# A ring of five places for U and ten for V, with row constants loaded per tile

## The chip, the cores and the metric

The kernel runs on one core of a Trainium2 chip. The metric is the device time of one execution in microseconds. A core has five engines, each with an instruction stream of its own: TensorE (PE, matrix products), VectorE (DVE), ScalarE (ACT), GpSimd (POOL) and SyncE (SP). Sixteen DMA engines serve the core; here GpSimd issues the gathers and SyncE nearly all the other loads. The engines meet only through semaphores.

## The reference, cut to what matters

Two transformer-like layers over one sequence of 512 tokens, width 1024, in float32. Layer 1 mixes with an S5 state space model and a banded attention, layer 2 with a compressed and a windowed attention and a short convolution. Each layer ends in the same step, which sets most of the traffic: every token picks 8 x 16 = 128 of 16384 experts, and each expert is one row of `u_tab` and one of `v_tab` (4 KB each).

```python
def block_fn(args):
    xb, eb, gb = args
    a = jnp.einsum('cd,ced->ce', xb, u_tab[eb]).astype(jnp.float32)
    w = (gb * jax.nn.gelu(a, approximate=False)).astype(xb.dtype)
    return jnp.einsum('ce,ced->cd', w, v_tab[eb])
```

`xb` is the normed row of the token times a row of gains: `ln2_g` in layer 1, and in layer 2 `ln_ffn_g_2` times one plus a modulation row, with another modulation row added. The output of layer 2 is normed once more with `ln_final_g_2`.

## The kernel before, in words

The tokens are cut into four tiles of 128, one token per partition, and the program goes through eight tiles in order: n = 0 to 3 are layer 1, n = 4 to 7 are layer 2 on the same tokens. A tile needs 128 **slots**; slot s = 128 n + k handles expert k of all 128 tokens of tile n. There are 1024 slots (`NSLOT`), and each engine's stream has a part for a slot:

- GpSimd gathers the U and the V row of the slot for every partition in one indirect DMA of 8 KB per partition, 1.05 MB in all (L1944). `both_rows(s)` gives the destination in the tile `ring`.
- VectorE multiplies U with the token's row and sums (`dot`, L372), which writes `aw`.
- ScalarE applies GELU and makes a diagonal matrix of the weights (`weigh`, `diag`; four buffers for diagonals, two slots at a time).
- TensorE adds diagonal times V into PSUM (`vmm`, L1472, 8 matmuls per slot). It takes V of slot c - `VL` when its stream is at slot c; `VL` is 4.

The ring has `NU` = 4 places for U and `NV` = 8 for V, so the gather of slot s waits for `dot(s - 4)` and for `vmm(s - 8)`, which is in TensorE's stream at its slot s - 4.

Beside the slots each stream holds the dense work of the *next* tile. `L1_PARTS` and `L2_PARTS` give the order and the width in slots: in layer 1 norm 4, win 25, qk 7, mid 52, branch 14, route 11, top 15; in layer 2 norm 4, win 30, conv 7, cmp 17, att 36, wout 7, route 12, top 15. `pace(n, part, f)` emits all slots that are due before that point of the part, so the position of each dense instruction among the slots is written into the stream of each engine, and every engine runs its stream strictly in order. In `mid` four groups g of 13 slots each do a head group of the attention and a quarter of the state space model. There TensorE comes in group g to `T.wait_ge("a_pt1", n, g)` at 13 g + 9 and waits until VectorE, in its own stream, has reached the copy of L678 (`att_pt`) at about the same slot.

The dense weights come through `wsl`, six buffers of two 128 x 512 blocks (`NWS`, 512 KB a unit). SyncE issues unit k when unit k - 6 has been used; `extra(k)`, called ahead of unit k, issues whatever other load belongs there, some after a wait. All of SyncE's loads are in one stream too. In layer 2 the units of a tile are 24 of `win`, 8 of `wout`, 8 of `wq` and 1 of `sk`; TensorE takes them in pairs (`project`), one slot between two pairs.

The constant rows lie in SBUF tiles of their own before the change: `rowA` holds the gain row of `route` (loaded once a layer), `gt1` the modulation row of the output projection (a part of `pers`, loaded once), `finr` the row of the last norm (loaded once). `fin`, 4 KB per partition, holds the output tile of layer 2 between `finish` and the store, parts of the state space work in layer 1, and half of the scores of `route`. `finish2(n - 1)` (the last norm's product) is emitted at slot `VL` + 4 of a tile. `kT1` holds the keys of all four tiles of layer 1.

Of the kernel before, what the change touches and what calls it, by code (L numbers as in the profile page):

```python
# [9 lines left out]
F32 = mybir.dt.float32  # L10
# [5 lines left out]
W1 = 384  # L16
NU = 4
NV = 2 * NU
NWS = 6
NSLOT = 1024  # L20
PAIR = 2
VL = 4
END = NSLOT + VL + 6

# [75 lines left out]
def build(nc, A, out, act_counts):  # L100
    ctx = ExitStack()
    with ctx:
# [50 lines left out]
        gt2 = sb("gt2", [128, D])  # L153
        finr = sb("finr", [128, D])
        xT = sb("xT", [128, 8, 128])
# [3 lines left out]
        cols3 = sb("cols3", [128, 2, 8])  # L159
        rowA = sb("rowA", [128, D])  # L160
        rowB = sb("rowB", [128, D])
        big = sb("big", [128, 5120])
        pers = sb("pers", [128, 13312])
        rflat = ring[:, :, :].rearrange("p a b -> p (a b)")
# [3 lines left out]
        L2d = nc.dram_tensor("L2d", [8, 16, W1], F32, kind="Internal").ap()  # L168
        modd = nc.dram_tensor("modd", [12, 512], F32, kind="Internal").ap()
        modr = modd.rearrange("(a b) c -> a (b c)", b=2)  # L170

# [10 lines left out]
        bias1, o = carve(pers, o, 16, 256)  # L182
        kT1, o = carve(pers, o, 2, 512)
        v1, o = carve(pers, o, 2, 256)
# [4 lines left out]
        snk, o = carve(pers, o, 16)  # L189
        assert o <= 13312, o  # L190

# [36 lines left out]
        zprev, o = carve(pers, o, 512)  # L228
        gt1, o = carve(pers, o, 1024)
        at_route = o  # L230
# [25 lines left out]

        rsc2 = finr[:, :]
        bmod = finr[:, 256:768].rearrange("p (b c) -> p b c", c=128)

        def route_bufs(blk):  # L260
            if blk:
                sS, o = carve(pers, at_route, 16, 128)
                halves, base = [sS[:, 0:8, :], sS[:, 8:16, :]], pers
            else:
                halves = [x[:, :].rearrange("p (a b) -> p a b", b=128) for x in (fin, gt2)]
                base, o = rowB, 0
            r = {"halves": halves}
            r["s2"], p = carve(base, o, 256)
            r["cand"], p = carve(base, p, 16, 16)
            r["oh"], o = carve(base, o, 2, 16, 16)  # L270
# [4 lines left out]
            assert o <= (13312 if blk else D), o  # L275
            return r
# [18 lines left out]
        assert o <= 3328  # L295
        mrow = [finr[:, 0:128], finr[:, 128:256]]
        first = [carve(rflat, 512 * k, 4, 128)[0] for k in range(3)]
# [64 lines left out]
        def vector_program(v):  # L362
# [28 lines left out]
            def finish2(n):  # L391
                V.stage("fin")
                V.wait_ge("fsq", n)
                V(v.tensor_scalar(st[:, 2:3], st[:, 2:3], 1.0 / D, 1e-6, ALU.mult, ALU.add))
                V.wait_own()
                V(v.reciprocal(st[:, 2:3], st[:, 2:3]), ("frc", n))
                V.wait_ge("frs", n)
                V.wait_ge("finr")
                V(v.scalar_tensor_tensor(fin[:, :], fin[:, :], st[:, 2:3], finr[:, :], ALU.mult, ALU.mult),
                  ("fout", n))  # L400

            def slots(x):
                back = V.here
                while V.slot < x and V.slot < END:
                    c = V.slot
                    V.slot += 1
                    n, k = divmod(c, 128)
                    if c < NSLOT:
                        dot(c)
                    if k == VL + 2 and n >= 1:  # L410
                        finish(n - 1)
                    if k == VL + 4 and n >= 5:
                        finish2(n - 1)
                V.stage(back)
# [156 lines left out]
            def qk1(n):  # L571
                i = n
                pace(n, "qk", 0.0)
                if n:
# [22 lines left out]
                V.wait_ge("kT_t", n)  # L597
                V(ts(kT1[:, :, 128 * i:128 * i + 128], PS[2][:, 0:256].rearrange("p (a b) -> p a b", a=2), kgc,
                     None, ALU.mult, None), ("kT", n))
# [181 lines left out]
            def route(n):  # L781
                i, blk, b = n % 4, n // 4, n % 2
                X = xn[:, b, :]
                pace(n, "route", 0.0)
                V.stage("route")
                rstd(n, "r", 1, D)
                if n == 4:
                    V.wait_ge("lnf")
                    V.wait_ge("modrow", 4)
                    V(v.scalar_tensor_tensor(rowA[:, :], rsc2, 1.0, rowA[:, :], ALU.add, ALU.mult), ("rowA", 1))  # L790
                    V.wait_own()
                if n == 0:
                    V.wait_ge("rowA", 0)
                V(v.scalar_tensor_tensor(X, hres[:, i, :], st[:, 1:2], rowA[:, :], ALU.mult, ALU.mult),
                  *([] if blk else [("X", n)]))
# [12 lines left out]
                pace(n, "route", 1.0)  # L808
# [238 lines left out]
            def wout2(n):  # L1047
# [19 lines left out]
                for b in range(2):  # L1067
# [4 lines left out]
                    V.wait_ge("wout", n, b)  # L1072
                    V.wait_ge("modrow", 2)
                    V(tt(x, PS[4 + b], gt1[:, 512 * b:512 * b + 512], ALU.mult), ("wo_e", n, b))
# [48 lines left out]
        def scalar_program(a):  # L1123
# [58 lines left out]
            def slots(x):  # L1182
                back = S.here
                while S.slot < x and S.slot < END:
# [7 lines left out]
                    if k == VL + 3 and n >= 5:  # L1192
                        finish(n - 1)
                    if k == VL + 4 and n >= 5:
                        finish2(n - 1)
# [118 lines left out]
            def route(n):  # L1314
# [141 lines left out]
        def tensor_program(t):  # L1456
# [143 lines left out]
            def scores1(n, g):  # L1600
# [8 lines left out]
                for r in range(4):  # L1609
                    k0 = 128 * (n - 1) + s0  # L1610
                    x = t.matmul(PS[r // 2][:, 256 * (r % 2) + s0:256 * (r % 2) + 256],
                                 xT[64 * a_:64 * a_ + 64, 4 * m + r, :],
                                 kT1[64 * a_:64 * a_ + 64, m, k0:128 * (n + 1)], start=True, stop=True)
                T(x, ("a_sc", n, g))
# [334 lines left out]
        def sync_program(s):  # L1949
# [20 lines left out]
            def extra(k):  # L1970
# [7 lines left out]
                if (n, name, b, u) == (0, "glu", 0, 0):  # L1978
                    load(rowA[:, :], A["ln2_g"].broadcast_to([128, D]), "rowA", 0)
                    load(shm[:, :, :], A["k_shift"], "shm")  # L1980
# [28 lines left out]
                if n >= 4 and (name, b, u) == ("win", 4, 0):  # L2009
                    Y.wait_ge("h", n - 1, 1)  # L2010
                    Q(s.dma_start(cw, A["conv_w_2"][0, :, 0, :].unsqueeze(0).broadcast_to([128, 3, 512])), "cw",
                      ("cw", n))
# [9 lines left out]
                if (n, name, b, u) == (5, "win", 0, 0):  # L2022
                    Y.wait_ge("rowA", 1)
                    load(finr[:, :], A["ln_final_g_2"].unsqueeze(0).broadcast_to([128, D]), "finr")

# [144 lines left out]
```

## Time and profile before

| | us |
|---|---|
| median of 3 runs | 3549.24 |
| lowest and highest | 3537.84, 3552.84 |
| the profiled execution | 3552.45 |
| its span | 3551.0 |
| PE busy | 2498.8 |
| DVE busy | 2390.7 |
| ACT busy | 1370.3 |
| POOL busy | 1078.5 |

The span goes from the first to the last instruction of the profiled execution. The program moved 1343.61 MB at a mean of 378 GB/s. A "DMA share" is the mean busy share of the 16 DMA engines; packets of two queues overlap a little in the records, so that a full stretch reads 1.00 to 1.02. Slots start at about 285 us; before that the first tile's dense work runs alone. In a timeline row the figures are start, length, engine, line, operation and, in brackets, how long the engine sat idle before it and what ended that.

### The profile page before, as it was taken

To read this page: it belongs to the slowest core of one execution; us is meant where nothing else is said; L and a number is where in the kernel's file an instruction comes from. 1 tells how busy PE (TensorE), PEld (TensorE's weight loads), DVE (VectorE), ACT (ScalarE), POOL (GpSimd) and SP (SyncE) were. 2 spreads that over 40 slices of the span, in tenths; PEclk is the share of its full clock that TensorE was granted. 3 is DMA by queue.
4 is the path that set the end of the run, shared out by engine and by line. 5 is a ranking of instruction groups with operands and counts; after the bars stand their busy time and mean duration, and the time that the engine had idled before them with its cause. 6 is when DMAs were issued, how large, how long until landed. Compare 5 with 4: busy or idle time off the path is not lost.

```text
span 3551.0 us, 40113 instructions
## 1 busy us (share of the span) xinstructions
PE 2498.8 (70%) x13640; PEld 977.6 (28%) x13640; DVE 2390.7 (67%) x5690; ACT 1370.3 (39%) x3648; POOL 1078.5 (30%) x1038
## 2 busy tenths in 40 slices
PE   7768669676696776866577667767677668765555
PEld 3433233222332223322222223222232223311111
DVE  7438873687835878467664886668775887666664
ACT  1113332344323443233283335534383436533332
POOL 0001332223322233332333323332333323333332
PEclk9689779798797987988778888888888888977777
DMA  7659999999999999999999999999999999999998
GB/s 241 218 200 375 369 355 406 416 408 393 359 396 416 416 391 355 385 394 396 380 409 395 399 398 394 395 400 414 374 401 393 393 394 401 387 386 393 396 407 336
DMA packets 228013, 1343.61 MB, mean 378 GB/s; under 512 B 28360, under 2 KB 33768, under 8 KB 95968
## 3 DMA queue, kind: packets, MB, share of 16 engines
q0 software_dynamic: 148320, 1076.50, 76.0%
q1 hardware_dynamic: 78816, 262.43, 19.3%
q8 instruction: 107, 1.75, 0.2%
q10 hardware_dynamic: 672, 2.12, 0.1%
q14 instruction: 98, 0.80, 0.1%
HBM read 1338.24 MB, written 2.71 MB: 378 GB/s over the span
## 4 chain that ended last, share of the span: by engine, by line
DMA 31%; PE 26%; DVE 17%; issue 15%; POOL 5%; ACT 4%; SPq 0%; POOLq 0%; ACTq 0%; DVEq 0%
DMA ring<-in_k_uv,idx 15%; PE ps L1543 12%; DMA ring<-in_k_vu,idx 12%; PE ps L1472 9%; DVE ring L372 6%; POOL ring L1944 5%; DMA wsl<-in_k_wu 4%; DVE big L420 2%; ACT L1128 1%; PE ps L1525 1%; PE ps L1681 1%; DVE rowB L420 1%; ACT diag L1128 1%; ACT xr L1128 1%; PE ps L1627 1%
## 5 line engine op out<-in xcount | busy, mean ns | idle before, releaser
L372 DVE CUSTOM_DVE_ANT_0 ring<-ring,xn 128x1024 f32<-128x1024 f32 x1024 | 1243.7, 1222 | 654.3 <-DMA ring<-in_k_uv,idx 351.7
L1472 PE MATMUL ps<-ring,diag 64*64 64x512 f32 x8192 | 1272.2, 741 | 518.9 <-ACT diag L1128 474.9
L1944 POOL DMA_INDIRECT ring<-in_k_vu,idx x512 | 530.7, 1036 | 1267.2 <-DVE aw L372 673.7
L1944 POOL DMA_INDIRECT ring<-in_k_uv,idx x512 | 541.7, 1058 | 1109.5 <-DVE aw L372 855.9
L1543 PE MATMUL ps<-wsl,xT 128*128 128x512 f32 (+1 forms) x1536 | 730.1, 622 | 77.9 <-DMA wsl<-in_k_wu 54.1
L1472 PEld LDWEIGHTS ps<-ring,diag 64*64 64x64 f32 x8192 | 304.8, 158 | 1240.8 <-ACT diag L1128 725.2
L1128 ACT ACTIVATE aw<-aw 128x2 f32<-128x2 f32 x512 | 103.9, 203 | 1320.1 <-DVE aw L372 1314.6
L1128 ACT ACT_TABLE_LOAD x375 | 481.1, 1283 | 64.2 <-DVE big L420 51.8
L1543 PEld LDWEIGHTS ps<-wsl,xT 128*128 128x128 f32 x1536 | 291.7, 200 | 528.1 <-issue 437.8
L1128 ACT ACTIVATE diag<-gid,aw 128x64 f32<-128x64 f32 x1024 | 306.3, 341 | 129.6 <-PE ps L1472 112.9
L1128 ACT ACTIVATE gid<-ident,gate 128x64 f32<-128x64 f32 x1024 | 292.5, 332 | 0.0
L1681 PE MATMUL ps<-pers,rowB 128*128 128x64 f32 x224 | 51.3, 421 | 106.1 <-DVE rowB L678 81.6
L1525 PE MATMUL ps<-ident,big 128*128 128x128 f32 x288 | 60.1, 332 | 81.9 <-DVE big L420 31.7
L420 DVE TENSOR_TENSOR big<-ps,big 128x512 f32<-128x512 f32 x40 | 27.6, 690 | 107.6 <-PE ps L1543 107.3
L1525 PE MATMUL ps<-ident,xr 128*128 128x128 f32 x208 | 37.1, 334 | 85.7 <-DVE xr L424 64.4
L372 DVE DVE_READ_ACCUMULATOR2_ANT aw<- 128x1 f32 x1024 | 83.9, 82 | 0.0
L1681 PEld LDWEIGHTS ps<-pers,rowB 128*128 128x128 f32 x224 | 48.7, 329 | 118.4 <-issue 118.4
L1525 PEld LDWEIGHTS ps<-ident,big 128*128 128x128 f32 x288 | 38.0, 164 | 137.3 <-ACT big L1128 60.6
L1128 ACT ACTIVATE xr<-ps 128x512 f32<-128x512 f32 x32 | 18.2, 589 | 144.6 <-PE ps L1543 141.1
L420 DVE TENSOR_TENSOR big<-big 128x512 f32<-128x512 f32 x84 | 58.2, 693 | 20.0 <-ACT big L1128 17.1
L1863 PE MATMUL ps<-pers,big 128*128 128x64 f32 x320 | 48.9, 288 | 23.9 <-DVE big L1024 23.9
L420 DVE TENSOR_TENSOR big<-ps,pers 128x512 f32<-128x512 f32 (+5 forms) x120 | 58.1, 494 | 3.5 <-PE ps L1627 2.8
(227 smaller groups left out, 2033.9 us busy)
## 6 DMA issues: line engine op xcount, KB each, us to landing
wsl<-in_k_wu SPq DMA_DIRECT2D x408, 512.0 KB
wsl<-in_k_wmod SPq DMA_DIRECT2D x48, 512.0 KB
ring<-in_k_vu,idx POOLq DMA_INDIRECT x512
ring<-in_k_uv,idx POOLq DMA_INDIRECT x512
wsl<-in_k_wu SPq DMA_DIRECT2D x16, 280.0 KB
big<-in_b_gate SPq DMA_DIRECT2D x4, 1024.0 KB, 11.7
big<-in_conv_w SPq DMA_DIRECT2D x4, 768.0 KB
hres<-in_x SPq DMA_DIRECT2D x4, 512.0 KB, 7.7
```

The costliest lines, as they stand in the source:

```text
L372: V(v.tensor_tensor_reduce(u_row(s), u_row(s), xn[:, b, :], 1.0, 0.0, ALU.mult, ALU.add, aw[:, b, k:k + 1]), ("dot", s))
L420: return v.tensor_tensor(out, a_, b_, op)
L1128: return a.activation(out, in_, f, **kw)
L1472: r = t.matmul(PA[half][64 * q:64 * q + 64, :], diag[64 * half:64 * half + 64, s % (2 * PAIR), :], v_row(s)[64 * half:64 * half + 64, 512 ...
L1525: r = t.transpose(PS[bank][:, j * 128:(j + 1) * 128], s_, ident[:, :])
L1543: r = t.matmul(PS[bank][:, 0:nn], lhsT(kk_), wsl[:, at % NWS, j, 0:nn], start=(kk_ == 0), stop=(kk_ == nk - 1))
L1627: x = t.matmul(PS[2 + b][:, 256 * h + 128 * z:256 * h + 128 * z + 128], BT[32 * j:32 * j + 32, 4 * z + c, :], uT[32 * j:32 * j + 32, c, :] ...
L1681: x = t.matmul(PS[4 + h // 8][:, 64 * (h % 8):64 * (h % 8) + 64], PT1[:, r, 128 * k:128 * k + 128], v1[:, (n + 1 + k) % 2, 64 * g:64 * g + ...
L1863: r = t.matmul(PS[4 + br][:, 64 * h:64 * h + 64], PT2[:, k % 2, 128 * j:128 * j + 128], vsn[:, j, 128 * br + 64 * g:128 * br + 64 * g + 64 ...
L1944: Q(p.indirect_dma_start(out=both_rows(s), out_offset=None, in_=tab, in_offset=bass.IndirectOffsetOnAxis(ap=idx[:, n % 2, k:k + 1], axis=0 ...
```

## The change

`NU` goes from 4 to 5, `NV` = 2 `NU` with it from 8 to 10, and `VL` from 4 to 5. The gather of slot s now waits for `dot(s - 5)` and `vmm(s - 10)`, and the latter stands in TensorE's stream at its slot s - 5. The three more places of 4 KB per partition come from elsewhere: `rowA` and `finr` are gone, and `pers` shrinks from 13312 to 12192 elements.

- The row of `route` is now `lnr`, a name for `fin`, loaded ahead of the first `wq` unit of every tile: 8 loads of 512 KB in place of 2. VectorE waits for it at the start of `route`. In tile 4 VectorE makes the product with the modulation row and ScalarE writes it to DRAM (`lnd`, 4 KB); tiles 5 to 7 load it from there.
- `gt1` lies in scratch space and is loaded in each tile of layer 2, ahead of the fifth `wout` unit and after a wait of SyncE for `o1`, the end of the attention: 4 loads in place of 1.
- The row of the last norm goes to `xr` or to `wsl`: 3 loads in place of 1, two of them ahead of the 17th `win` unit of tiles 6 and 7 with a wait for `perm`, the end of an earlier tile's sum. `finish2` moves to slot 20.
- `kT1` keeps two tiles of keys; for even n the score matmul over 256 columns becomes two over 128.

```diff
-NU = 4
+NU = 5
 NV = 2 * NU
+PERS = 12192
-VL = 4
+VL = 5
...
-                    if k == VL + 4 and n >= 5:
+                    if k == (20 if n < 8 else VL + 4) and n >= 5:
                         finish2(n - 1)
...
                 rstd(n, "r", 1, D)
+                V.wait_ge("lnr", n)
                 if n == 4:
-                    V.wait_ge("lnf")
                     V.wait_ge("modrow", 4)
-                    V(v.scalar_tensor_tensor(rowA[:, :], rsc2, 1.0, rowA[:, :], ALU.add, ALU.mult), ("rowA", 1))
+                    V(v.scalar_tensor_tensor(lnr, rsc2, 1.0, lnr, ALU.add, ALU.mult), ("lnf",))
...
+                if n == 4:
+                    S.wait_ge("lnf")
+                    Q(a.dma_start(lnd, lnr[0:1, :]), "lnd", ("lnd",))
...
+                    if n % 2:
+                        x = t.matmul(PS[r // 2][:, 256 * (r % 2):256 * (r % 2) + 256], q,
+                                     kT1[64 * a_:64 * a_ + 64, m, :], start=True, stop=True)
+                    else:
+                        for k in range(s0 // 128, 2):
+                            x = t.matmul(PS[r // 2][:, 256 * (r % 2) + 128 * k:256 * (r % 2) + 128 * k + 128], q,
+                                         kT1[64 * a_:64 * a_ + 64, m, 128 * (1 - k):256 - 128 * k],
+                                         start=True, stop=True)
...
-                    load(rowA[:, :], A["ln2_g"].broadcast_to([128, D]), "rowA", 0)
...
-                    load(rsc2, modr[4:5, :].broadcast_to([128, 1024]), "modrow", 4)
-                    Y.wait_ge("X", 3)
-                    load(rowA[:, :], A["ln_ffn_g_2"].broadcast_to([128, D]), "lnf")
...
-                    load(gt1, modr[2:3, :].broadcast_to([128, 1024]), "modrow", 2)
...
+                if n >= 4 and (name, b, u) == ("wout", 1, 0):
+                    Y.wait_ge("o1", n, 1)
+                    Q(s.dma_start(gt1, modr[2:3, :].broadcast_to([128, 1024])), "gt1", ("gt1", n))
+                    if n == 4:
+                        load(rsc2, modr[4:5, :].broadcast_to([128, 1024]), "modrow", 4)
+                if (name, b, u) == ("wq", 0, 0):
+                    if n < 4:
+                        Y.wait_ge("s5b", n, 1)
+                        row = A["ln2_g"]
+                    elif n == 4:
+                        Y.wait_ge("gate", 3, 7)
+                        row = A["ln_ffn_g_2"]
+                    else:
+                        Y.wait_ge("lnd")
+                        if n >= 6:
+                            Y.wait_ge("out", n - 2)
+                        row = lnd
+                    Q(s.dma_start(lnr, row.broadcast_to([128, D])), "lnr", ("lnr", n))
+                if n >= 6 and (name, b, u) == ("win", 4, 0):
+                    last_row(n - 2)
+
+            def last_row(*tiles):
+                if tiles[0] < 6:
+                    Y.wait_ge("perm", tiles[0])
+                Q(s.dma_start(finr(tiles[0]), A["ln_final_g_2"].unsqueeze(0).broadcast_to([128, D])), "finr",
+                  *[("finr", n) for n in tiles])
```

## Rows read from the trace of the kernel before

**Rows 1.** the page: busy share of the 16 DMA engines in 40 slices; SyncE's queue.

```profile
DMA  7659999999999999999999999999999999999998
...
q1 hardware_dynamic: 78816, 262.43, 19.3%
```

**Rows 2.** windows by stage: PE, PEld, DVE, ACT, POOL busy; TensorE clock, DMA share, GB/s.

```profile
375.00:529.00 154.00, 95.10 (x650) 46.76 (x650) 123.65 (x225) 56.88 (x178) 53.02 (x52) 0.77 0.92 362
...
829.00:979.00 150.00, 95.28 (x656) 45.67 (x656) 123.53 (x226) 58.41 (x180) 53.91 (x53) 0.77 0.93 369
...
1278.00:1432.00 154.00, 97.30 (x664) 47.49 (x664) 122.69 (x224) 57.16 (x177) 56.34 (x53) 0.76 0.91 358
...
1879.00:1949.00 70.00, 55.91 (x280) 21.84 (x280) 33.24 (x59) 21.06 (x64) 23.08 (x19) 0.95 0.97 389
...
1949.00:2105.00 156.00, 104.44 (x504) 35.22 (x504) 129.99 (x384) 61.30 (x164) 47.79 (x48) 0.88 1.01 407
...
2105.00:2180.00 75.00, 48.91 (x386) 23.04 (x389) 49.76 (x102) 23.54 (x79) 27.21 (x27) 0.77 0.92 366
...
2268.00:2341.00 73.00, 60.66 (x304) 22.86 (x296) 35.57 (x68) 24.74 (x71) 23.71 (x20) 0.92 0.98 393
...
2498.00:2572.00 74.00, 48.88 (x379) 23.08 (x379) 49.95 (x104) 22.52 (x75) 28.60 (x27) 0.77 0.93 367
...
2663.00:2738.00 75.00, 61.65 (x307) 23.50 (x306) 36.12 (x68) 24.85 (x71) 22.74 (x20) 0.91 0.99 392
...
2895.00:2970.00 75.00, 49.83 (x380) 23.28 (x380) 51.09 (x108) 23.66 (x76) 30.30 (x27) 0.77 0.94 370
...
3062.00:3130.00 68.00, 57.20 (x292) 21.86 (x284) 32.79 (x60) 23.33 (x69) 24.20 (x20) 0.95 0.93 360
...
3130.00:3440.00 310.00, 172.22 (x940) 40.96 (x944) 214.09 (x522) 103.25 (x334) 122.89 (x118) 0.74 0.99 399
...
3440.00:3520.00 80.00, 44.78 (x256) 10.13 (x248) 39.26 (x63) 19.18 (x76) 29.64 (x32) 0.76 1.01 415
```

**Rows 3.** waits of GpSimd, 285 to 3551 us: total, times, longest.

```profile
POOL ring L1944 <- DVE aw L372: 1529.6, 605, 34.2
POOL ring L1944 <- PE ps L1472: 538.3, 213, 16.4
```

**Rows 4.** timeline of one stall: start, length, engine, operation, idle before it.

```profile
436.20 0.94 POOL L1944 DMA_INDIRECT ring<-in_k_vu,idx  x1 [1.06 <-DVE aw L372]
...
437.43 3.65 PE L1681 MATMUL ps<-pers,rowB 128*128 128x64 f32 x16 [9.40 <-DVE rowB L678]
...
441.01 4.77 PE L1472 MATMUL ps<-ring,diag 64*64 64x512 f32 x32
...
443.80 0.94 POOL L1944 DMA_INDIRECT ring<-in_k_vu,idx  x1 [6.67 <-DVE aw L372]
```

**Rows 5.** window of two microseconds in that stall.

```profile
444.00:446.00 2.00, 2.00 (x21) 0.62 (x14) 1.97 (x3) 0.82 (x3) 1.70 (x2) 1.00 0.43 74
```

**Rows 6.** timeline of a stall in the convolution stage of a second-layer tile.

```profile
2113.53 1.22 DVE L372 CUSTOM_DVE_ANT_0 ring<-ring,xn 128x1024 f32<-128x1024 f32 x1
...
2115.03 1.68 POOL L1944 DMA_INDIRECT ring<-in_k_vu,idx  x1 [4.63 <-DVE aw L372]
```

**Rows 7.** timeline of the output projection of tile 5.

```profile
2268.25 0.69 DVE L420 TENSOR_TENSOR big<-big 128x512 f32<-128x512 f32 x1
...
2286.21 0.69 DVE L420 TENSOR_TENSOR xr<-ps,pers 128x512 f32<-128x512 f32 x1 [4.23 <-PE ps L1543]
...
2287.13 3.70 PE L1543 MATMUL ps<-wsl,xT 128*128 128x512 f32 x8
...
2299.66 1.28 DVE L794 SCALAR_TENSOR_TENSOR xn<-hres,st,rowA 128x1024 f32<-128x1024 f32 x1 [1.16 <-ACT st L1128]
```

**Rows 8.** DMA issues: count, size, median us from issue to landing.

```profile
finr<-in_ln_final_g SPq DMA_DIRECT2D x1, 512.0 KB, 15.8
```

**Rows 9.** groups of TensorE in the middle stage of tile 2: busy, mean ns.

```profile
L1611 PE MATMUL ps<-pers,xT 64*128 64x256 f32 x24 | 6.0, 389 | 0.0
```

More of the change, by code:

```diff
@@ L153, in build @@
         gt2 = sb("gt2", [128, D])
-        finr = sb("finr", [128, D])
         xT = sb("xT", [128, 8, 128])
@@ L159, in build @@
         cols3 = sb("cols3", [128, 2, 8])
-        rowA = sb("rowA", [128, D])
         rowB = sb("rowB", [128, D])
         big = sb("big", [128, 5120])
-        pers = sb("pers", [128, 13312])
+        pers = sb("pers", [128, PERS])
         rflat = ring[:, :, :].rearrange("p a b -> p (a b)")
@@ L169, in build @@
         modd = nc.dram_tensor("modd", [12, 512], F32, kind="Internal").ap()
+        lnd = nc.dram_tensor("lnd", [1, D], F32, kind="Internal").ap()
         modr = modd.rearrange("(a b) c -> a (b c)", b=2)
@@ L182, in build @@
         bias1, o = carve(pers, o, 16, 256)
-        kT1, o = carve(pers, o, 2, 512)
+        kT1, o = carve(pers, o, 2, 256)
         v1, o = carve(pers, o, 2, 256)
@@ L189, in build @@
         snk, o = carve(pers, o, 16)
-        assert o <= 13312, o
+        mrow = [carve(pers, o + 128 * k, 128)[0] for k in range(2)]
+        bmod, o = carve(pers, o + 256, 4, 128)
+        assert o <= PERS, o
         gt, o = carve(big, 0, 2048)
@@ L228, in build @@
         zprev, o = carve(pers, o, 512)
-        gt1, o = carve(pers, o, 1024)
         at_route = o
@@ L248, in build, with finr @@
         tmp2, o = carve(big, o, 512)
+        gt1, _ = carve(big, o2 + 1024, 1024)
+        lnr = fin[:, :]
+        def finr(n):
+            return xr[:, :] if n < 6 else wsl[:, 0, :, :].rearrange("p a b -> p (a b)")
         gg = cols2[:, 0:24]
@@ L255, in build @@
         o3 = o1r.rearrange("p (h d) -> p h d", d=64)
-        rsc2 = finr[:, :]
-        bmod = finr[:, 256:768].rearrange("p (b c) -> p b c", c=128)
+        rsc2, _ = carve(big, o2, 1024)
         def route_bufs(blk):
@@ L274, in route_bufs @@
                 r[nm], o = carve(base, o, *shape, dt=dt)
-            assert o <= (13312 if blk else D), o
+            assert o <= (PERS if blk else D), o
             return r
@@ L295, in build @@
         assert o <= 3328
-        mrow = [finr[:, 0:128], finr[:, 128:256]]
         first = [carve(rflat, 512 * k, 4, 128)[0] for k in range(3)]
@@ L397, in finish2 @@
                 V.wait_ge("frs", n)
-                V.wait_ge("finr")
-                V(v.scalar_tensor_tensor(fin[:, :], fin[:, :], st[:, 2:3], finr[:, :], ALU.mult, ALU.mult),
+                V.wait_ge("finr", n)
+                V(v.scalar_tensor_tensor(fin[:, :], fin[:, :], st[:, 2:3], finr(n), ALU.mult, ALU.mult),
                   ("fout", n))
@@ L597, in qk1 @@
                 V.wait_ge("kT_t", n)
-                V(ts(kT1[:, :, 128 * i:128 * i + 128], PS[2][:, 0:256].rearrange("p (a b) -> p a b", a=2), kgc,
+                V(ts(kT1[:, :, 128 * (i % 2):128 * (i % 2) + 128], PS[2][:, 0:256].rearrange("p (a b) -> p a b", a=2), kgc,
                      None, ALU.mult, None), ("kT", n))
@@ L786, in route @@
                 rstd(n, "r", 1, D)
+                V.wait_ge("lnr", n)
                 if n == 4:
-                    V.wait_ge("lnf")
                     V.wait_ge("modrow", 4)
-                    V(v.scalar_tensor_tensor(rowA[:, :], rsc2, 1.0, rowA[:, :], ALU.add, ALU.mult), ("rowA", 1))
+                    V(v.scalar_tensor_tensor(lnr, rsc2, 1.0, lnr, ALU.add, ALU.mult), ("lnf",))
                     V.wait_own()
-                if n == 0:
-                    V.wait_ge("rowA", 0)
-                V(v.scalar_tensor_tensor(X, hres[:, i, :], st[:, 1:2], rowA[:, :], ALU.mult, ALU.mult),
+                V(v.scalar_tensor_tensor(X, hres[:, i, :], st[:, 1:2], lnr, ALU.mult, ALU.mult),
                   *([] if blk else [("X", n)]))
@@ L1072, in wout2 @@
                     V.wait_ge("wout", n, b)
-                    V.wait_ge("modrow", 2)
+                    V.wait_ge("gt1", n)
                     V(tt(x, PS[4 + b], gt1[:, 512 * b:512 * b + 512], ALU.mult), ("wo_e", n, b))
@@ L1193, in slots @@
                         finish(n - 1)
-                    if k == VL + 4 and n >= 5:
+                    if k == (20 if n < 8 else VL + 4) and n >= 5:
                         finish2(n - 1)
@@ L1609, in scores1 @@
                 for r in range(4):
[L1610 to L1613, printed above, removed]
+                    q = xT[64 * a_:64 * a_ + 64, 4 * m + r, :]
+                    if n % 2:
[6 more added lines that the diff above has]
+                                         start=True, stop=True)
                 T(x, ("a_sc", n, g))
@@ L2010, in extra @@
                     Y.wait_ge("h", n - 1, 1)
+                    if n == 5:
+                        Y.wait_ge("lnf")
                     Q(s.dma_start(cw, A["conv_w_2"][0, :, 0, :].unsqueeze(0).broadcast_to([128, 3, 512])), "cw",
@@ L2021, in extra @@
                     load(gt2[:, :], modr[5:6, :].broadcast_to([128, 1024]), "modrow", 5)
-                if (n, name, b, u) == (5, "win", 0, 0):
-                    Y.wait_ge("rowA", 1)
-                    load(finr[:, :], A["ln_final_g_2"].unsqueeze(0).broadcast_to([128, D]), "finr")
+                if n >= 4 and (name, b, u) == ("wout", 1, 0):
[23 more added lines that the diff above has]
+                  *[("finr", n) for n in tiles])
             load(hres[:, 0, :], A["x"][0, 0:128, :], "x", 0)
@@ L2041, in sync_program @@
                 unit(k)
+            for k in range(len(units) - NWS, len(units)):
+                Y.wait_ge("unit_used", k)
+            last_row(6, 7)
         for engines in ((Blank(),) * 5, (nc.vector, nc.scalar, nc.tensor, nc.gpsimd, nc.sync)):
```

## The prediction

> **What bounds the kernel now.** I read the page's slices first, for what is full nearly all the time. From the fourth slice on the 16 DMA engines are busy 90% or more of every slice but none of the compute engines is [rows 1]. Then I read the windows by stage [rows 2], because a mean hides where the DMA engines do run dry. In full stages the share reads 1.01 (1949 to 2105 us, mostly `win` of tile 5, and the closing slots, 3440 to 3520 us). In the latter only gathers run: 32 in 80 us, so one gather of 1.05 MB costs 2.5 us of all DMA engines. Against 1.01 the dry time is share lost times length [rows 2]:
>
> - `mid` of tiles 1, 2, 3: 0.09 x 154 + 0.08 x 150 + 0.10 x 154 = 41.3 us;
> - `conv` and `cmp` of tiles 5, 6, 7: 0.09 x 75 + 0.08 x 74 + 0.07 x 75 = 17.9 us;
> - `wout` and `route` of tiles 4 to 7: 0.04 x 70 + 0.03 x 73 + 0.02 x 75 + 0.08 x 68 = 11.9 us;
> - 3130 to 3440 us: 0.02 x 310 = 6.2 us.
>
> Together 77.3 us. The time after 285 us is bytes over a fixed rate plus this dry time, so an edit can win only by closing dry time, and loses by bytes.
>
> Who opens it? GpSimd waits 1529.6 us for dots and 538.3 us for TensorE's reading of V [rows 3]. Most of that is harmless: with full queues the gather of s + 4 can't be issued before the dot of s, which itself waits for data. What hurts is a gap between two issues longer than the data in flight lasts. One such gap is in [rows 4]: TensorE sits 9.40 us at L1681 until VectorE has made the copy of L678, then works off four V slots from 441.01 us on. VectorE comes late because it first has dots to do in its stream. Gathers were issued at 436.20 us and then not before 443.80 us. (The row names a dot as releaser, but the next V is free only as TensorE's block of 441.01 proceeds, so I take it as V.) From 444 to 446 us the DMA share is 0.43 and 74 GB/s move [rows 5]. `mid` has four such groups, three tiles, so 12 stalls, 41.3 / 12 = 3.4 us each. In the convolution stage VectorE itself is late: it reaches its dot at 2113.53 us behind dense work, and the next gather leaves at 2115.03 us after 4.63 us of idle GpSimd [rows 6]; there the dot is the gate. Neither kind is a rate limit: VectorE is busy 123.65 of 154 us in `mid`, 80%, and TensorE 95.10 [rows 2].
>
> **The change, part by part. The ring.** Take the stall of [rows 4]. TensorE stands at its slot P and has read V up to P - 5; before, GpSimd may gather up to P - 5 + 8 = P + 3. After, TensorE has read up to P - 6 and GpSimd may gather up to P - 6 + 10 = P + 4. Of the two places that V gains, `VL` takes one back. The dot's gate moves by one as well, from s - 4 to s - 5. So at each stall of either kind one more gather is in flight, 2.5 us of DMA work. A stall that runs dry for 3.4 us keeps 0.9 us; one that runs dry for less closes. The end of TensorE's stall does not move: it is VectorE's arrival at L678. That TensorE runs one slot further ahead only makes its wait start earlier.
>
> Gain in `mid`: at most 12 x 2.5 = 30 us. I take 28, because the shortened stage asks VectorE to be busy 123.65 / 144 = 86%, and some latency now hidden by the wait for data will show. In `conv` and `cmp` there are two stalls a tile, six of 17.9 / 6 = 3.0 us; at most 15 us. I take 11, because SyncE now holds back `wout` units 5 and 6 (below), whose 2 x 1.37 us of traffic came just ahead of the first of them and covered part of it. `wout` and `route`: 11.9 us in about eight small stalls; I take 6. The close: 2 of 6.2 us. Sum 47 us. The bounds are 0 (each stall grows by what the ring gains) and all 77.3.
>
> **The loads.** 15 broadcast loads in place of 4, so 11 more of 0.524 MB. SyncE's queue moved 262.43 MB in 19.3% of the 3551 us of all engines [rows 1], 2.61 us per MB, so 1.37 us a load and 15.1 us in all. They fall into `branch`, `wout`, `route` and `win`, which are nearly full, so I take all 15.1; if the dry time of `wout` and `route` hides four of them, 9.6 is left.
>
> **The waits.** SyncE waits for `o1` ahead of the fifth `wout` unit. Queued behind it: `gt1`, units 5 to 8, `lnr`, the `wq` units. In tile 5 `o1` ends at 2268.25 + 0.69 = 2268.94 us; `gt1` is wanted at 2286.21, 17.3 us later, unit 5 at 2287.13, 18.2 us later [rows 7]. A load of this size took 15.8 us from issue to landing in full traffic [rows 8]; into an otherwise empty SyncE queue it should take less. `lnr` goes out when the first pair of units is used, some 4 pairs ahead of the norm's product at 2299.66 us [rows 7], about 18 us as well. So each is just in time by one row. Units 5 and 6 come behind `gt1`; at bad luck they are late by two transfers at, say, a third of the 415 GB/s, 2 x 0.524 / 0.138 = 7.6 us, less the 18.2 - 15.8 = 2.4 of margin: 5 us. While TensorE waits for them the DMA engines are loading them, so the time isn't lost unless GpSimd runs out of places too; I take 0.5 us in each of four tiles, 2 us, bounds 0 and 20. The waits for `perm` in tiles 6 and 7 hold weights for about four slots and let them catch up; 1 us together, bounds 0 and 5. Behind VectorE's wait for `lnr` stand the dots, but five gathers (12.5 us) lie ahead of them. The waits for `lnd`, `s5b` and `out` are met long before.
>
> **At nothing.** The even tiles' second score matmul: 16 more in tile 2, each at most the 389 ns of the wide one [rows 9], 6 us at most on a TensorE that is busy 95.28 of 150 us there [rows 2]; if its cover went, 3 us. The 4 KB store and the later `finish2` hang on nothing that is waited for; the tail after the last gather has the same instructions.
>
> Sum against the profiled execution: 3552.45 - 47 + 15.1 + 3 = 3523.5 us. It lies 3.2 us above the median of the runs, so the forecast for the median is 3520 us, 0.8% less.
>
> **A rule of the skill, weighed.** In [rows 8] a SyncE load takes 15.8 us to land while gathers of 2.5 us each fill the other queue. The Trainium skill, page "DMA: Bandwidth & Descriptors", section "Queues, rings and completion order", says that each DMA engine goes round-robin between the queues that have work, switching at packets. By that rule a fifth gather in flight costs SyncE's loads nothing; if both queues were served in the order of issue, each burst of loads would stand 2.5 us longer. The row doesn't decide it.
>
> **The rivals.**
> *Stalls grow with the ring.* TensorE's wait starts a slot earlier, ScalarE's four diagonals now wait for `vmm(s - 4)` at one slot later of TensorE's stream, and the work that follows the stall shifts too. If only a third of the gain comes, 15 us, it pays the traffic and no more: 3549 us, up to 3564 with no gain. For it: [rows 3] show TensorE as the gate in 213 waits. Against it: the stall's end in [rows 4] hangs on VectorE's dots alone, and those on data.
> *SyncE's held queue becomes the bound* (the slower side). It decides from the point where `gt1` with two units takes over 18.2 us from `o1`. Then TensorE is late in four tiles by 5 us, V places stay shut, `lnr` makes VectorE late in turn, and 20 us come on top of 15.1, against a gain cut to 10 by the same weights missing ahead of `conv`: 3549 + 25 = 3574 us. For it: the 15.8 us of [rows 8]. Against it: `wout` and `route` are dry for 11.9 us today, so late weights find room.
> *Queues in order of issue.* A burst of loads waits 2.5 us longer, in seven tiles 17.5 us of TensorE's time; 3520 + 17.5 = 3537 us. Nothing in the rows speaks for it but the 15.8.
>
> **How the numbers follow.** A change of 0.5% is 17.7 us; less can't be told from none. The forecast 0.62, with a range of its own from 3500 (some 59 us that one gather a stall can close, 9.6 paid) to 3534. Stalls that grow 0.22. The held queue 0.10. Order of issue 0.06. Faster by over 0.5% is nearly all of the first: 0.61. Same is the last, most of the second, the edge of the first: 0.27. Slower 0.12. The range for 8 in 10 starts at 3487 (77.3 us closed, 9.6 + 3 paid gives 3485) and ends at 3558, inside the second case, leaving out the held queue.
>
> **What would show it.** `mid` of tiles 1 to 3 down from 154, 150 and 154 us by about 9 each, with DMA shares of 0.97 or more; no gap of over 7 us between two gathers there that takes the share under 0.5; `conv` and `cmp` at 71 to 73 us; `win` of layer 2 no shorter; q1 up by 5.8 MB. TensorE's wait at L1681 stays or grows while the stage shrinks. The forecast is wrong if the `mid` shares stay at 0.92, if VectorE is found waiting on `fin` (`lnr`) or TensorE on `wsl` in `wout`, or if the share there falls.

## The result, and the profile after

The changed kernel takes 3452.78 us (median of 4 runs, 3451.2 to 3454.39) against 3551.04 us for the kernel before on the same chips: ratio 0.9725, 95% interval 0.9692 to 0.9759. That is 98 us less; 29 were forecast. The profiled execution took 3452.99 us with a span of 3451.5.

The page of the changed kernel, the lines that answer to [rows 1], with the rate in each slice:

```profile
DMA  7669999999999999999999999999999999999997
...
GB/s 243 212 220 374 401 385 407 415 388 409 394 405 416 417 393 390 405 415 408 377 419 415 415 394 406 415 417 413 394 419 416 415 397 418 417 408 420 419 419 328
...
q0 software_dynamic: 148320, 1076.50, 76.8%
...
q1 hardware_dynamic: 80400, 268.20, 20.2%
```

The gathers' queue on the page before:

```profile
q0 software_dynamic: 148320, 1076.50, 76.0%
```

The sixteen engines still read "9" nearly everywhere, and SyncE's queue moved 268.20 MB, 5.77 more, as the loads say. For the same 1076.50 MB the gathers' packets took 0.760 x 3551.0 = 2699 us of all engines before and 0.768 x 3451.5 = 2651 us after: 48 us less. So a packet was recorded as shorter on average, and a busy share can't show such a gain. The readings of the DMA share have moved little; the GB/s have moved more. That is where the prediction went wrong, so here is the stretch from 300 to 3400 us of both kernels, before and then after (columns as in [rows 2]; the last two are DMA share and GB/s):

```profile
300.00:3400.00 3100.00, 2200.66 (x12286) 846.49 (x12290) 2143.86 (x5067) 1276.64 (x3391) 1016.70 (x967) 0.83 0.98 393
```

```profile
300.00:3400.00 3100.00, 2202.50 (x12618) 849.33 (x12618) 2193.88 (x5182) 1308.39 (x3485) 1083.52 (x1005) 0.84 1.00 408
```

The share rises by 0.02, the rate by 15 GB/s. The closing slots of [rows 2] reach 415 GB/s, so take 415 as full. By bytes the kernel before was dry for 3100 x (1 - 393/415) = 164 us, and the changed one for 3100 x (1 - 408/415) = 52 us. The difference is 112 us, less 13.9 us for 5.77 MB more: 98 us. (That this meets the measured 98 proves nothing: with the same bytes but for the loads, a shorter time is a higher rate. And "dry" here means below 415 GB/s, whatever the reason.) Of the 112 us the share shows 0.02 x 3100 = 62. The other 50 lie inside time that it counts as busy.

The stages of the changed kernel that answer to [rows 2] (cut at its own slots; `mid` of tiles 1, 2, 3; `conv` and `cmp` of tile 5; its attention, 2118 to 2212; `conv` and `cmp` of 6 and 7; `wout` and `route` of 7; then most of the last slots):

```profile
369.00:509.00 140.00, 96.01 (x672) 46.52 (x668) 122.53 (x226) 58.52 (x179) 58.42 (x52) 0.79 0.99 394
...
814.00:953.00 139.00, 92.98 (x668) 46.63 (x664) 121.79 (x224) 57.43 (x176) 57.77 (x52) 0.77 0.99 397
...
1254.00:1395.00 141.00, 96.09 (x668) 46.76 (x664) 122.55 (x225) 58.45 (x179) 55.94 (x53) 0.79 0.98 393
...
2058.00:2118.00 60.00, 41.03 (x358) 20.56 (x360) 40.18 (x84) 19.16 (x65) 27.71 (x24) 0.78 0.93 373
...
2118.00:2212.00 94.00, 69.65 (x422) 28.61 (x414) 64.70 (x139) 77.67 (x169) 36.54 (x37) 0.84 1.01 417
...
2443.00:2502.00 59.00, 40.59 (x363) 20.70 (x361) 40.41 (x85) 19.21 (x65) 27.51 (x23) 0.79 0.95 384
...
2829.00:2887.00 58.00, 40.20 (x360) 19.41 (x358) 40.32 (x84) 19.39 (x65) 28.11 (x24) 0.79 0.96 393
...
2980.00:3044.00 64.00, 53.07 (x264) 21.32 (x268) 33.00 (x60) 21.91 (x64) 19.11 (x17) 0.97 1.01 406
...
3084.00:3417.00 333.00, 186.55 (x1072) 44.87 (x1076) 217.05 (x488) 107.42 (x365) 135.65 (x134) 0.77 1.01 419
```

`mid` goes from 362, 369 and 358 GB/s to 394, 397 and 393, and from 154, 150 and 154 us to 140, 139 and 141: 38 us where I had 28. The windows of `conv` and `cmp` can't be set against the 75, 74 and 75 us of [rows 2] in this way: they hold 23 or 24 gathers, those 27. Cut at the starts of the same slots' dots in both traces, `conv` and `cmp` of tiles 5 to 7 take 190 us before and 177 after. Two stages that I had called full or almost full gained as well, though. Before, the attention of tile 5 and the last slots looked like this, cut at the same slots:

```profile
2177.00:2273.00 96.00, 71.73 (x422) 28.05 (x414) 64.98 (x140) 77.87 (x169) 36.28 (x37) 0.82 1.01 413
3170.00:3516.00 346.00, 191.10 (x1068) 45.51 (x1064) 217.25 (x487) 106.22 (x361) 134.84 (x133) 0.75 1.00 402
```

At a share of 1.01 and 1.00 they moved 413 and 402 GB/s; afterwards 417 and 419, in 2 and 13 us less.

One stall of `mid`, the place of [rows 4], in the changed kernel (timeline: start, length, engine, operation, idle before it):

```profile
423.65 0.94 POOL L1956 DMA_INDIRECT ring<-in_k_vu,idx  x1 [1.55 <-DVE aw L378]
...
424.88 3.65 PE L1693 MATMUL ps<-pers,rowB 128*128 128x64 f32 x16 [6.87 <-DVE rowB L684]
...
428.45 5.84 PE L1479 MATMUL ps<-ring,diag 64*64 64x512 f32 x32
...
431.24 1.16 POOL L1956 DMA_INDIRECT ring<-in_k_vu,idx  x1 [6.66 <-DVE aw L378]
```

GpSimd's gap of 6.66 us (before 6.67) is still there, and so is TensorE's wait for L684 (before L678), now 6.87 us. By the gates one more gather is in flight ahead of the gap. The windows in and behind it show what that does:

```profile
429.00:431.00 2.00, 2.00 (x12) 0.49 (x8) 1.97 (x5) 0.49 (x3) 0.00 (x0) 0.50 1.02 422
431.00:433.00 2.00, 2.00 (x16) 0.70 (x12) 1.97 (x3) 0.77 (x4) 1.21 (x2) 0.53 0.81 336
```

In place of 0.43 and 74 GB/s [rows 5] the lowest of these is 0.81 and 336 GB/s. The waits from 285 us on (total, times, longest):

```profile
POOL ring L1956 <- DVE aw L378: 1391.9, 578, 33.0
...
POOL ring L1956 <- PE ps L1479: 502.5, 203, 17.2
...
ACT diag L1132 <- PE ps L1479: 420.4, 206, 14.8
...
PE ps L1550 <- DMA wsl<-in_k_wu: 115.1, 52, 16.2
```

GpSimd waits for dots and TensorE about as long as in [rows 3]. ScalarE's wait for a free diagonal grew from 112.9 us before to 420.4, and TensorE's for weights from 49.3 to 115.1. Some 40 us of the latter lie in `win` of tiles 5 to 7, where the longest are 4.3, 5.6 and 5.7 us; in `a_old_gates`, with the same loads and waits of SyncE but the old gates, the total is 50.9. What the wait for diagonals costs, the runs with VL 4 bound.

The output projection of tile 5, in answer to [rows 7]:

```profile
2207.49 0.69 DVE L426 TENSOR_TENSOR big<-big 128x512 f32<-128x512 f32 x1
...
2208.22 0.33 SPq L2033 DMA_DIRECT2D big<-modd  x1
...
2227.70 0.69 DVE L426 TENSOR_TENSOR xr<-ps,big 128x512 f32<-128x512 f32 x1 [3.95 <-PE ps L1550]
...
2228.61 3.70 PE L1550 MATMUL ps<-wsl,xT 128*128 128x512 f32 x8
...
2241.15 1.28 DVE L798 SCALAR_TENSOR_TENSOR xn<-hres,st,fin 128x1024 f32<-128x1024 f32 x1 [1.16 <-ACT st L1132]
```

`gt1` is issued at 2208.22 us, when `o1` ends. It is used at 2227.70, and the third pair of units starts at 2228.61, 20.4 us after `o1` and straight behind its slot. The norm's product finds its row in `fin`. SyncE's wait for `o1` holds nobody up in this tile.

### The profile page after: what moved, and what is told of

It reads as the page before. It is cut to its first block, busy times and chain, and to the rows that moved or that the text cites. A ratio compares the mean times of both kernels' runs of the same rounds, so it can differ in the third digit from the quotient of the medians.

```text
span 3451.5 us, 40205 instructions
## 1 busy us (share of the span) xinstructions
PE 2444.3 (71%) x13672; PEld 965.6 (28%) x13672; DVE 2384.9 (69%) x5690; ACT 1376.0 (40%) x3646; POOL 1107.7 (32%) x1038
## 3 DMA queue, kind: packets, MB, share of 16 engines
q0 software_dynamic: 148320, 1076.50, 76.8%
q1 hardware_dynamic: 80400, 268.20, 20.2%
## 4 chain that ended last, share of the span: by engine, by line
DMA 32%; PE 30%; DVE 14%; issue 12%; ACT 6%; POOL 4%; POOLq 0%; ACTq 0%; DVEq 0%
PE ps L1550 13%; DMA ring<-in_k_uv,idx 11%; DMA ring<-in_k_vu,idx 11%; PE ps L1479 10%; DMA wsl<-in_k_wu 9%; DVE ring L378 5%; POOL ring L1956 4%; ACT L1132 2%; PE ps L1532 1%; PE ps L1797 1%; PE ps L1693 1%; DVE big L426 1%; ACT diag L1132 1%; ACT gid L1132 1%; PE ps L1639 1%
## 5 line engine op out<-in xcount | busy, mean ns | idle before, releaser
L1479 PE MATMUL ps<-ring,diag 64*64 64x512 f32 x8192 | 1221.4, 719 | 301.0 <-ACT diag L1132 280.2
L1956 POOL DMA_INDIRECT ring<-in_k_vu,idx x514 | 552.3, 1075 | 1179.0 <-DVE aw L378 695.8
L1956 POOL DMA_INDIRECT ring<-in_k_uv,idx x510 | 549.3, 1077 | 1066.2 <-DVE aw L378 696.1
L1132 ACT ACTIVATE diag<-gid,aw 128x64 f32<-128x64 f32 x1024 | 317.6, 343 | 435.7 <-PE ps L1479 420.4
L1693 PE MATMUL ps<-pers,rowB 128*128 128x64 f32 x224 | 49.9, 413 | 95.5 <-DVE rowB L684 59.6
L1875 PE MATMUL ps<-pers,big 128*128 128x64 f32 x320 | 49.3, 290 | 27.6 <-DVE big L1028 27.0
```

Of the source, the lines that this page charges most:

```text
L1132: return a.activation(out, in_, f, **kw)
L1479: r = t.matmul(PA[half][64 * q:64 * q + 64, :], diag[64 * half:64 * half + 64, s % (2 * PAIR), :], v_row(s)[64 * half:64 * half + 64, 512 ...
L1693: x = t.matmul(PS[4 + h // 8][:, 64 * (h % 8):64 * (h % 8) + 64], PT1[:, r, 128 * k:128 * k + 128], v1[:, (n + 1 + k) % 2, 64 * g:64 * g + ...
L1875: r = t.matmul(PS[4 + br][:, 64 * h:64 * h + 64], PT2[:, k % 2, 128 * j:128 * j + 128], vsn[:, j, 128 * br + 64 * g:128 * br + 64 * g + 64 ...
L1956: Q(p.indirect_dma_start(out=both_rows(s), out_offset=None, in_=tab, in_offset=bass.IndirectOffsetOnAxis(ap=idx[:, n % 2, k:k + 1], axis=0 ...
```

## The experiments

All ratios are to the kernel before, timed on the same chip. Medians are in us.

**The old gates in the new layout.** Everything but the depth stays changed:

```diff
-VL = 5
+VL = 4
...
-                    G.wait_ge("dot", s - NU)
+                    G.wait_ge("dot", s - 4)
...
-                    G.wait_ge("vmm", s - NV)
+                    G.wait_ge("vmm", s - 8)
```

> The changed kernel with the old gates: a gather waits for dot(s - 4) and vmm(s - 8), VL is 4; the rows loaded per tile, finish2 at slot 20 and the two-tile keys stay. Theory 1 (the gain is the fifth gather alone, and the loads cost what their bytes cost): before plus 15 us, 3560 to 3570 us, ratio to before 1.003 to 1.006. Theory 2 (a good part of the 98 us comes from what was moved beside the ring: the held units, the later finish2, the constant rows): under 3535 us, ratio under 0.996.

3551.51, ratio 0.9999 (0.9979 to 1.0019). Neither number came. There is no gain, so what was moved beside the ring brings none of the 98 us, within 0.2%, unless it pays for a cost of the loads; and no loss, so the loads cost nothing here, with the same reserve. The next run takes the loads away. Nor is it TensorE's clock: the granted clock was 0.839 in this profile and 0.842 in the changed kernel's. Its 300 to 3400 us:

```profile
300.00:3400.00 3100.00, 2181.05 (x12318) 841.56 (x12314) 2146.88 (x5078) 1275.89 (x3392) 1005.86 (x966) 0.85 0.98 395
```

395 GB/s in place of 393: the added bytes went into dry time.

**Narrow rows.** Do the loads cost anything, and is it hidden by something else? `lnr` of tiles 1 to 3 and 5 to 7 and `gt1` of 5 to 7 load 64 of 1024 columns (the rest of the row is left as it lies, so this part of the computation is left out):

```diff
+                    wd = D if n in (0, 4) else 64
-                    Q(s.dma_start(lnr, row.broadcast_to([128, D])), "lnr", ("lnr", n))
+                    Q(s.dma_start(lnr[:, 0:wd], row[:, 0:wd].broadcast_to([128, wd])), "lnr", ("lnr", n))
```

With the old gates:

> The same narrow rows with the old gates and VL 4. With the wide rows it was 3551.5 us, as the kernel before. Theory A (the dry time of the old gates takes the loads in, for nothing): 3548 to 3552 us. Theory B (the loads cost 15 us there too and something else of the new layout, the later finish2 or SyncE's order, gives 15 back): 3535 to 3540 us.

3553.0, ratio 1.0003 (0.9986 to 1.002), the same as with the wide rows: theory A, a microsecond above its range. So no cost of the loads is hidden there. With the new gates:

> The changed kernel; lnr in tiles 1, 2, 3, 5, 6, 7 and gt1 in tiles 5, 6, 7 load only 64 of 1024 columns (the rest keeps what lies there), so 9 of the 11 added loads are nearly gone. Theory A (with the queues full, bytes cost their 1.37 us each): 12 us faster than the changed kernel, 3438 to 3444 us. Theory B (they are hidden): within 4 us of 3453.

3449.2 (3438.26 to 3455.83), ratio 0.9706 (0.9669 to 0.9744) against 0.9725 (0.9692 to 0.9759). The median lies in theory B's range, but the intervals hold both 0 and 12 us, so this run doesn't settle what the loads cost where little dry time is left.

**The square of the two gates.** At VL 4, which gate carries the gain? `c_v_gate8` has dot(s - 5), vmm(s - 8); `k_u4_vl4` has dot(s - 4), vmm(s - 10); `d_vl4` has both new:

> The changed kernel, but a gather waits for vmm(s - 8) and VL is 4; the dot's gate stays at s - 5. Theory 1: the stalls of mid come back (12 of them at 2.5 to 3.4 us) and TensorE's lag caps the depth at other places too: 3500 to 3550 us. Rival (the dots' gate alone carries the gain): under 3475 us.

> The changed kernel with VL 4, a gather waits for dot(s - 4) and vmm(s - 10): the fourth corner of a square at VL 4 with a_old_gates (4 and 8: 3551.5), c_v_gate8 (5 and 8: 3513.8) and d_vl4 (5 and 10: 3435.7). Theory 1 (both gates close the same stalls, a stall needs both open, so the gains do not add): V's two places alone bring 20 to 40 us, 3510 to 3530, while the two together bring 116, more than the sum of the two. Rival (the gains add): 3551.5 - (3513.8 - 3435.7) = 3473 us.

> The changed kernel with VL back at 4, gates s - 5 and s - 10. V is read one slot earlier in TensorE's stream, so V gains two gathers of reach at a stall in place of one. Theory 1 (depth is all): the V-gated stalls that are left close too, 3435 to 3453 us. Rival (VL = 5 is itself part of the gain, since TensorE waits less for ScalarE's diagonals): slower than the changed kernel, 3460 to 3490 us.

| VL 4 | vmm(s - 8) | vmm(s - 10) |
|---|---|---|
| dot(s - 4) | 3551.5 | 3508.8 (ratio 0.9896, 0.9878 to 0.9914) |
| dot(s - 5) | 3513.8 (0.9901, 0.9879 to 0.9924) | 3435.7 (0.9673, 0.9652 to 0.9693) |

Each gate alone brings 38 to 43 us, both together 116: 35 us more than the sum (by the ratios 44). That fits a gather having to pass both. Both theory 1's came in kind; V's gate alone ended a microsecond under its range. `d_vl4` also shows that VL 5 is no part of the gain but costs some 17 us: the same ring with VL 4 is faster than the changed kernel (3431.75 to 3436.08 against 3451.2 to 3454.39; the intervals of the two ratios just touch). In its trace, from 285 to 3400 us, GpSimd waits 252.7 us for TensorE where the changed kernel has 496.2, and ScalarE 131.3 us for a free diagonal where that has 420.4; which of the two makes the 17 us wasn't tried. Its 300 to 3400 us, at 410 GB/s:

```profile
300.00:3400.00 3100.00, 2236.38 (x12674) 851.95 (x12674) 2198.29 (x5196) 1306.19 (x3503) 1105.66 (x1012) 0.85 1.01 410
```

**The dot's gate alone set back, with VL 5:**

> The changed kernel, but a gather waits for dot(s - 4); V keeps ten places and VL 5. Theory 1 (both gates must be one deeper, since with full queues the dot's gate sets how many gathers are in flight): most of the gain goes, 3530 to 3560 us. Rival (V places were what opened the stalls, as I read in mid): most of the gain stays, under 3490 us.

3521.4, ratio 0.9911 (0.9887 to 0.9934): 69 of the 98 us go, most of the gain as theory 1 had it, though 9 us under its range. At VL 4 the same gates take 3508.8.

**Shallower.** How does the price run with depth?

> The same with dot(s - 3), vmm(s - 10), VL 4: with k_u4_vl4 and d_vl4 a row of the dot's depth 3, 4, 5 at the same VL and V places. Theory 1 (the cost rises faster with each gather taken away, because at 3 a gather's own landing, its dot and the next issue no longer fit in the time of the others): 3700 to 3850 us. Rival (equal steps, as 2.5 us a stall would give): 3590 to 3620 us.

3864.8, ratio 1.0905 (1.0875 to 1.0934): theory 1, and 15 us beyond it. With the dot's gate at 3, 4 and 5 (vmm(s - 10), VL 4) the kernel takes 3864.8, 3508.8 and 3435.7: steps of 356 and 73 us. All gates shallower, with VL 3:

> The changed kernel with gates dot(s - 3) and vmm(s - 6) and VL 3: one step shallower than the old gates, in the same layout. Theory 1 (each stall costs what the data in flight do not cover; one gather is 2.5 us, and a dry queue costs more than its dry time because the first packets after it are slow): the step from 3 to 4 is worth at least the 98 us of the step from 4 to 5, 3650 to 3750 us. Rival (the 98 us are a threshold crossed at 5, for example of TensorE's and ScalarE's coupling): 3570 to 3610 us.

3992.3, ratio 1.1229 (1.1183 to 1.1275), more than either number, but VL 3 has a price of its own, as the next run shows.

**VL 3.**

> The changed kernel with VL 3, gates s - 5 and s - 10. Theory 1: V gates reach two slots further than with VL 5, but the dot's gate at s - 5 already sets the depth at VL 4 nearly everywhere; little more is left, and TensorE may now wait for ScalarE's diagonals within a slot: 3428 to 3445 us. Rival (TensorE's reading of V is still what opens most stalls): under 3425 us. Second rival (the wait for the diagonals decides): over 3450 us.

3496.4, ratio 0.9845 (0.9812 to 0.9879), 61 us above `d_vl4`: in the range of the second rival. TensorE's waits for a diagonal, from 285 to 3400 us, total 507.7 us where `d_vl4` has 379.5; that they make the 61 us isn't shown. The place is the attention of layer 2. A hundred microseconds of it, tile 6:

```profile
2500.00:2600.00 100.00, 81.00 (x430) 34.21 (x428) 61.25 (x135) 71.81 (x151) 38.44 (x32) 0.78 0.85 328
```

328 GB/s, where the changed kernel has 417 in such a stretch. Cut at the slots, the four attention stages take 448 us in place of `d_vl4`'s 374, and all else some 14 us less (my expectation below says 16). So V read 3 slots behind everywhere but there and in the first 8 slots of a tile:

> The changed kernel with V read 3 slots behind the dot outside the attention of layer 2, and 4 in it and in the first 8 slots of a tile. h_vl3 lost 74 us in that attention and won 16 elsewhere against d_vl4. If that is so: 3415 to 3425 us. Rival (the win elsewhere was only time passed on from the attention): 3434 to 3445 us.

3429.9, ratio 0.9653 (0.9633 to 0.9674), between the two ranges: beside `d_vl4`'s 0.9673 (0.9652 to 0.9693) no difference that this measurement can tell. It is the fastest median of the study, with `d_vl4` close behind; both beat the changed kernel.

**Gathers alone.** The disputed price by itself, one profiled execution:

> A kernel of gathers alone, the rest of the computation left out: phases of 40 gathers of 1.05 MB from the table of layer 1 (random rows), each phase drained before the next. Phases 1 to 5: a gather waits only for the landing K before it, K = 1 to 5. Then with the dot of 1.22 us between landing and the next issue, K = 2 to 5; then the same with 32 loads of 512 KB by SyncE beside the 40 gathers, K = 3 to 5. Theory 1 (a dry queue costs some 4 to 5 us from issue to the first data and slow first packets, full queues 2.5 us a gather): K = 1 at 6 to 8 us a gather, K = 2 at 3 to 4, K = 3 and more at 2.5; with the dot K = 3 at 2.6 to 3.0, K = 4 and 5 at 2.5, so that undisturbed depth 4 is enough and only stalls make 5 worth something. Rival (depth 4 is too little even undisturbed): K = 5 over 1% faster per gather than K = 4 in the phases with the dot.

Windows within the phases, first K = 1, 2, 3, 4 with the landing as the gate; then K = 2, 3, 4, 5 with the dot in the loop; then K = 3, 4, 5 with loads beside it (POOL's count in brackets is the number of gathers):

```profile
20.00:220.00 200.00, 0.00 (x0) 32.68 (x35) 1.00 0.54 182
...
250.00:345.00 95.00, 0.00 (x0) 30.90 (x33) 1.00 0.98 359
...
365.00:445.00 80.00, 0.00 (x0) 29.85 (x32) 1.00 1.01 417
...
470.00:545.00 75.00, 0.00 (x0) 28.55 (x31) 1.00 1.01 422
...
685.00:815.00 130.00, 40.69 (x66) 31.40 (x34) 1.00 0.79 272
...
845.00:950.00 105.00, 38.77 (x64) 29.97 (x32) 1.00 0.85 319
...
980.00:1055.00 75.00, 35.96 (x60) 28.24 (x30) 1.00 1.00 409
...
1085.00:1160.00 75.00, 37.12 (x62) 27.98 (x30) 1.00 1.01 422
...
1195.00:1310.00 115.00, 38.45 (x63) 29.18 (x32) 1.00 1.02 417
...
1345.00:1460.00 115.00, 37.85 (x61) 28.96 (x31) 1.00 1.02 418
...
1490.00:1600.00 110.00, 37.00 (x60) 27.40 (x29) 1.00 1.02 418
```

With the landing as gate: 200 / 35 = 5.7 us a gather, then 2.9, 2.5, 2.4. With the dot: 130 / 34 = 3.8, 105 / 32 = 3.3, 75 / 30 = 2.5 and 75 / 30 = 2.5, but 409 against 422 GB/s for the last two. By the gathers' issue times over 30 of them it is 2.54 and 2.48 us, 2% apart. With SyncE's loads beside them 417, 418 and 418 GB/s at 3, 4 and 5: there depth doesn't matter. Theory 1 was too high for K = 1, a little for K = 2, and too low for K = 3 with the dot. Two things follow, both from a single execution. Where gathers run alone, four places with a dot in the loop are 2 to 3% short even when nothing disturbs them: the rival of my expectation was right. And K = 2 shows a share of 0.98 with 359 GB/s, K = 4 one of 1.01 with 422. One gather of the first phase, issued at 25.57 us, shows how that comes:

```profile
25.57:27.20 1.63, 0.00 (x0) 0.93 (x1) 1.00 0.05 5
27.20:28.20 1.00, 0.00 (x0) 0.00 (x0) 1.00 1.02 197
28.20:30.60 2.40, 0.00 (x0) 0.00 (x0) 1.00 0.85 352
```

For 1.6 us, not the 4 to 5 of my expectation, next to nothing moves. Then the engines read as fully busy for a microsecond in which packets for only 197 GB/s begin: the first packets after an empty queue are recorded as long ones. In the windows above a packet of 8 KB is recorded with 385 ns on average at K = 1, 357 at K = 2 and 313 at K = 4. What the engine does in the longer ones isn't shown. (A full stretch reads 1.01 here with one queue alone, so the overlap of two queues' packets, named above, is not what lifts it over 1.00.)

**Where the gain lies.** The new gates only in `mid`, and everywhere but in `mid` (VL 4):

```diff
+                mid = any(place(m, "mid") <= s - 4 < place(m, "mid") + 52 for m in (1, 2, 3))
+                nu, nv = (5, 10) if mid else (4, 8)
```

> The changed kernel at VL 4 with the new gates (s - 5, s - 10) only for the gathers whose slots lie in mid of tiles 1 to 3, and the old ones (s - 4, s - 8) elsewhere. All old is 3551.5 us, all new 3435.7. Theory S (the stalls of mid hold most of it): 3480 to 3495 us. Theory W (every stage in which gathers run alone gains, mid is three stages of it): its 46 us of stage time and no more, 3500 to 3515 us.

> The reverse: the old gates in mid, the new ones elsewhere, VL 4. Theory S: 3490 to 3505 us. Theory W: 3475 to 3490 us. With p_mid_deep it also shows whether the places add: 3551.5 - p + 3551.5 - q = 116.

3505.5, ratio 0.9855 (0.9834 to 0.9877), and 3489.6, ratio 0.9818 (0.9796 to 0.9839). `mid` gives 46 us, all else 62, together 108 of 116. Theory W, with both medians in its ranges: `mid` holds 40%.

## Why the prediction was wrong

- **What bounds the kernel:** right. The time after 285 us is bytes over a rate plus dry time, and the ring closes dry time; `a_old_gates` with `g_old_gates_narrow` shows that nothing else in the change does. (The last of the 40 slices of [rows 1] reads 8, not 9; nothing hangs on it.)
- **The failed step: the dry time, "share lost times length", 77.3 us, and with it every stage that the share called full, priced at nothing.** Against 415 GB/s 164 us are lacking. The same rows had the right figure in their last column: `mid` at 362 of 415 GB/s lacks 19.7 us where 0.09 x 154 gave 13.9; 3130 to 3440 us at 399 lacks 12.0 us, where I had 6.2 and took 2. [rows 5] had shown it in small: a share of 0.43 with 74 GB/s, where 0.43 of 415 would be 178. Cut at the starts of the same slots' dots in the two traces, the terms of the sum measured: `mid` 38 us (I had 28), `conv` and `cmp` 13 (11), `wout` and `route` 5 (6), the last slots 14 (2). Together 70, where I had 47. Some 30 us more came from stages that I had at nothing: 12 in the attention of layer 2, 7 in its `norm`, the rest in `qk` and in `win`, `conv` and `cmp` of tile 4. These are differences between one trace each.
- **"At each stall one more gather, 2.5 us":** the mechanism is right, as the unmoved gap of 6.66 us shows, with a rate of 336 GB/s behind it in place of 74. The size was too small in two ways. `mid` gave 38 us in the changed kernel and 46 at VL 4, over 12 stalls 3.2 and 3.8 us each. The likely reason is that a queue that doesn't run dry also saves the long first packets; no run separates it from other, smaller gaps in `mid`. And I looked for stalls only; the loop of landing, dot and issue at depth 4 loses 2 to 3% where gathers run alone (`m_depth`). Between `a_old_gates` and `d_vl4` the attention of layer 2 shrinks by 14 of 387 us and the last slots by 9 of 359, which fits; `conv` and `cmp` of layer 2 shrink by 22 of 262, which is more than that loop explains. How the 62 us outside `mid` divide between loop and stalls wasn't tried by itself.
- **"`VL` takes one back":** right in direction: with VL 4 the kernel is 17 us faster, and GpSimd waits for TensorE half as long. ScalarE's wait for diagonals falls as well, so V's gate isn't shown to be all of it.
- **The loads, 15.1 us:** wrong as a cost. With the old gates they cost nothing within 0.2%, since dry time lay beside them. With the new gates 13.9 us is only what the bytes would take at 415 GB/s; the direct test couldn't tell it from nothing.
- **The waits, 3 us:** no clear cost. In tile 5 `lnr` and `gt1` are there in time, and the held queue rival fails at 20.4 us of room. In `wout` of tiles 4 and 5 the dots of seven slots take 3.4 and 2.3 us longer than before, in tiles 6 and 7 no longer; why wasn't tried. The weights came late in `win` of tiles 6 and 7, where SyncE waits for `perm` (5.6 and 5.7 us), and the stages are as long as before within 0.5 us.
- **Stalls that grow:** they didn't. TensorE's waits for VectorE's copy, which I had said would stay or grow, fell from 81.6 to 59.6 us. **Order of issue:** in the changed kernel SyncE's loads of 512 KB into `wsl` and `fin` landed in 11.8 to 15.8 us (medians), against the 15.8 of [rows 8]. No run isolates this.

The 0.61 was given to the right mechanism, but the range hung on 77.3 us as the most that could be won, and 98 came. Its lower bound rested on a measure that was itself too small.

## What to carry to other kernels

Measure the lost time of a DMA-bound kernel by bytes against the best rate that a stretch of the same kernel reaches, not by the busy share. A ring's depth has to cover landing, the consumer's instruction and the next issue, and then the longest gap between issues. Test it with the gathers alone, and deepen every gate in the loop: here one deeper gate without the other brought a third. When places are added, keep the consumer's lag as it was at first, and try the lag by itself: here 3 cost 61 us, 4 was best and 5 cost 17.

## What was unexpected of the hardware

The DMA share reads 0.98 at 359 GB/s and 1.01 at 422 in one kernel: the first packets after a dry queue are recorded as long ones, 197 GB/s at a share of 1.02. A single gather of 1.05 MB in flight takes 5.7 us from issue to the next issue, 2.3 times the 2.5 us of full queues. Beside loads of the other queue the depth of the gathers doesn't matter down to 3 (417 GB/s), though the same loop alone falls to 319. The price of depth is steep in this kernel: the third to fourth place of U is worth 356 us, the fourth to fifth 73.
